# Mixer stage of a two-block transformer kernel: score products in pairs, two banks for transposes, convolution taps spread, gate projections moved to the last round, exponentials after the probability copies

## What is computed

```python
proj = einsum('bsd,dn->bsn', rmsnorm(x), w_in)      # qa ka va za | qb kb vb ob zb | gates | ga gb
# branch A, 4 heads, two components of 64 features each
scores = q @ k.T * d**-0.5 + alibi_bias             # causal, block of 128 queries
p = softmax(scores)
p = p[:, :, 0] - lam * p[:, :, 1]                   # difference of the two components
oa = p @ v
# branch B (mLSTM), 4 heads of 128 features; q and k first go through a causal convolution of 4 taps and silu
Sm = (q @ k.T) * Dm ; num = Sm @ v + w_inter * (q @ C) ; den = ...
h = num / max(|den|, exp(-m)) ; C = decay * C + (wk * k).T @ v
# both outputs are later normalised and multiplied by silu(za), sigmoid(ob), silu(zb)
```

## Time and profile before

| | us |
|---|---|
| median of 3 runs | 2411.23 |
| lowest, highest | 2407.95, 2414.12 |
| the profiled execution, its own time | 2416.63 |
| its span, first to last instruction | 2414.8 |
| mixer stage on PE, first to last projection product | 1326.0 to 2014.5 |

### The profile page before, as it was taken

How to read it: one execution, slowest core, us unless ns; L and a number is a source line. 1 busy time by engine, 2 the same in 40 slices (tenths; PEclk the granted TensorE clock), 3 DMA queues, 4 the chain that set the end, 5 groups by cost and what they waited for, 6 DMA issues and landing times. The chain is left out here.

```text
span 2414.8 us, 29418 instructions
## 1 busy us (share of the span) xinstructions
PE 2131.7 (88%) x11320; PEld 1673.9 (69%) x11320; DVE 1240.3 (51%) x2222; ACT 866.5 (36%) x1364; POOL 251.8 (10%) x159
## 2 busy tenths in 40 slices
PE   3589999999999999679993999999899887999998
PEld 1467878787878777557772866667676655788877
DVE  5658586775858595547445334224233231633453
ACT  2365353535343434147113132433333442520121
POOL 0220202020201111000002211111111100000000
PEclk7789999999999999789996999999999898999999
DMA  6123232322222232156112210120211104311232
GB/s 280 37 74 98 59 104 63 97 92 69 92 66 87 72 94 66 47 203 213 46 44 97 65 53 27 53 79 27 93 38 35 61 26 183 98 50 46 86 92 83
DMA packets 126523, 199.21 MB, mean 82 GB/s; under 512 B 56325, under 2 KB 87813, under 8 KB 125233
## 3 DMA queue, kind: packets, MB, share of 16 engines
q1 hardware_dynamic: 126384, 197.34, 25.2%
HBM read 155.17 MB, written 42.11 MB: 82 GB/s over the span
## 5 line engine op out<-in xcount | busy, mean ns | idle before, releaser
L709 PE MATMUL p_job<-h_hi,w_hi 128*128 128x512 f32 x784 | 332.7, 424 | 45.5 <-DVE w_lo L850 22.9
L710 PE MATMUL p_job<-h_lo,w_hi 128*128 128x512 f32 x784 | 313.1, 399 | 0.0
L711 PE MATMUL p_job<-h_hi,w_lo 128*128 128x512 f32 x784 | 312.1, 398 | 0.0
L1697 PE MATMUL m_job<-h_hi,m_hi 128*128 128x512 f32 x592 | 263.3, 445 | 36.7 <-POOL m_lo L1533 36.7
L1699 PE MATMUL m_job<-h_hi,m_lo 128*128 128x512 f32 x592 | 240.2, 406 | 0.0
L1698 PE MATMUL m_job<-h_lo,m_hi 128*128 128x512 f32 x592 | 239.6, 405 | 0.0
L709 PEld LDWEIGHTS p_job<-h_hi,w_hi 128*128 128x128 f32 x784 | 151.8, 194 | 88.6 <-DVE w_lo L850 23.1
L710 PEld LDWEIGHTS p_job<-h_lo,w_hi 128*128 128x128 f32 x784 | 151.7, 193 | 37.4 <-issue 8.5
L711 PEld LDWEIGHTS p_job<-h_hi,w_lo 128*128 128x128 f32 x784 | 151.6, 193 | 32.8
L1697 PEld LDWEIGHTS m_job<-h_hi,m_hi 128*128 128x128 f32 x592 | 115.8, 196 | 82.9 <-POOL m_lo L1533 37.3
L1533 POOL TENSOR_TENSOR m_lo<-m_raw,m_hi 128x1024 fp32r<-128x1024 f32 x37 | 89.8, 2428 | 467.2 <-DVE m_hi L1805 467.2
(11 more groups left out here) (357 smaller groups left out, 4356.2 us busy)
## 6 DMA issues: line engine op xcount, KB each, us to landing
w_raw<-in_w SPq DMA_DIRECT2D x49, 512.0 KB, 3.6
m_raw<-in_w SPq DMA_DIRECT2D x37, 512.0 KB, 3.6
rows<-grows SPq DMA_DIRECT2D x32, 512.0 KB, 6.4
ada<-in_ada_w SPq DMA_DIRECT2D x8, 1536.0 KB, 12.6
e_raw<-in_w SPq DMA_DIRECT2D x24, 512.0 KB, 3.7
z_scr<-pre SPq DMA_DIRECT2D x16, 512.0 KB
o_scr<-oT SPq DMA_DIRECT2D x64, 128.0 KB, 1.8
ob<-o_scr SPq DMA_DIRECT2D x16, 512.0 KB, 3.7
```

What stands on the lines that cost most here:

```text
L709: nc.tensor.matmul(p_job[h][:], hi, h_hi[:, k, cut], start=(k == 0), stop=False)
L710: nc.tensor.matmul(p_job[h][:], hi, h_lo[:, k, cut], start=False, stop=False)
L711: last = nc.tensor.matmul(p_job[h][:], lo, h_hi[:, k, cut], start=False, stop=(k == KD - 1))
L1697: nc.tensor.matmul(p_job[h][:], hi, h_hi[:, k, cut], start=(k == 0), stop=False)
```

## The change

Nothing of the arithmetic changes; what changes is order, buffers and engines.

- **Score products in pairs.** A score step was (t, component) with all keys of the block. Now it is (t, a) with a the half of 512 keys: both components are multiplied one behind the other, component c into bank c of `p_sc`. The row minimum of a block with two halves is the smaller of two, a DVE instruction more. Twelve score steps a head for sixteen, with weight 2 + t%4.
- **Two transpose banks.** `p_t` becomes two banks used in turn; a cols or turn step waits for the copy of the one before the previous. The second bank is that of `p_a`, which moves into columns 128 to 255 of the bank of `p_s`; so apply waits for the state update of its block, and sim for the copy of the previous apply.
- **Exponentials behind the copies.** Both exponentials of block t+1 are a step `exps` of their own after the turns of block t. The second turn of a block stands behind the second score of the next one.
- **Taps spread.** Each of the four taps of qb and kb is a step `tap` of its own, dealt out 1, 3, 5 and 7 slices after the job; its silu comes at 10 slices.
- **Gates.** Rounds 1 to 3 have two gate jobs each, round 4 has six: 128, 128, 128 and 96 slices for 144, 144, 144 and 48.
- **The low part of the weights** is made by DVE directly after the high part; POOL keeps one instruction a round (line 1546).

```diff
+GATE_SHARE = (0, 2, 2, 2, 6)
...
-        steps += [("score", 0, 0), ("score", 0, 1), ("sim", 0)]
-        for i in range(NT):
-            steps += [("blend", i)]
-            if i + 1 < NT:
-                steps += [("score", i + 1, 0), ("score", i + 1, 1)]
-            steps += [("update", i)]
-            steps += [("turn", i, q) for q in range((i + 4) // 4)]
-            steps += [("apply", i), ("out", i)]
+        steps += [("score", 0, 0), ("exps", 0), ("sim", 0)]
+        for t in range(NT):
+            steps += [("blend", t)]
+            steps += [("score",) + x for x in SCORES if x == (t + 1, 0)]
+            steps += [("update", t), ("turn", t, 0)]
+            steps += [("score",) + x for x in SCORES if x == (t + 1, 1)]
+            steps += [("turn", t, 1)] if t >= 4 else []
+            steps += [("exps", t + 1)] if t + 1 < NT else []
+            steps += [("apply", t), ("out", t)]
...
         if s[0] == "score":
-            return 2 + s[1] // 3
+            return 2 + s[1] % 4
...
+                        behind += [(1 + 2 * q, ("tap", j, q)) for q in range(TAPS)] + [(10, ("silu", j))]
...
-        p_t, p_a, p_s, p_u = ps("p_t"), ps("p_a"), ps("p_s"), ps("p_u")
+        p_t = [ps("p_t0"), ps("p_t1")]
+        p_s, p_u = ps("p_s"), ps("p_u")
+        p_a = p_s[:, P:2 * P]
...
-                def split_lo(J):
-                    pool.wait_ge(w_hi_done, J + 1)
-                    nc.gpsimd.tensor_tensor(w_lo[:, J % 2, :], w_raw[:], w_hi[:, J % 2, :].bitcast(F32),
-                                            ALU.subtract).then_inc(w_lo_done, 1)
...
+                        elif s[0] == "exps":
+                            t = s[1]
+                            w = (t + 1) * P
+                            if NT * g + t >= 2:
+                                act.wait_ge(rl_done, 2 * (NT * g + t) - 2)
+                            for c in range(2):
+                                if t >= 4:
+                                    act.wait_ge(mn_done, NT // 2 * g + t - 3)
+                                else:
+                                    act.wait_ge(sc_used, NSC * g + 2 * o[("score", t, 0)] + c + 1)
+                                nc.scalar.activation(sc[:, t % 2, c, 0:w], sc[:, t % 2, c, 0:w], ACT.Exp, scale=-1.0,
+                                                     bias=mn[:, t % 2, 0, c:c + 1], accum_out=ls[:, t % 2, c:c + 1]
+                                                     ).then_inc(exp_done, 1)
...
                         elif s[0] == "score":
...
-                            w = (t + 1) * P
-                            half = slice(DA * c, DA * (c + 1))
-                            for a in range(0, w, HALF):
-                                e = min(a + HALF, w)
-                                last = nc.tensor.matmul(p_sc[:, a:e], qa[half, g % 2, t * P:(t + 1) * P],
-                                                        ka[half, g % 2, a:e], start=True, stop=True)
-                            last.then_inc(sc_ready, 1)
+                            a0, e = a * HALF, min((a + 1) * HALF, (t + 1) * P)
+                            for c in range(2):
+                                half = slice(DA * c, DA * (c + 1))
+                                nc.tensor.matmul(p_sc[:, c * HALF:c * HALF + e - a0], qa[half, g % 2, t * P:(t + 1) * P],
+                                                 ka[half, g % 2, a0:e], start=True, stop=True).then_inc(sc_ready, 1)
                         elif s[0] == "turn":
...
-                            if o[s]:
-                                pe.wait_ge(turn_cp, m)
+                            if o[s] >= 2:
+                                pe.wait_ge(turn_cp, m - 1)
...
                         elif s[0] == "apply":
...
+                            pe.wait_ge(c_done, (NT + 1) * g + 2 + t)
...
                         elif s[0] == "sim":
...
+                                pe.wait_ge(app_cp, m)
...
-                def split_hi(J):
+                def split(J):
                     dve.wait_ge(w_in, 16 * (J + 1))
                     if J >= 2:
                         dve.wait_ge(half_done, 2 * (J - 1))
                     nc.vector.tensor_copy(w_hi[:, J % 2, :], w_raw[:]).then_inc(w_hi_done, 1)
+                    dve.wait_ge(w_hi_done, J + 1)
+                    nc.vector.tensor_tensor(w_lo[:, J % 2, :], w_raw[:], w_hi[:, J % 2, :].bitcast(F32),
+                                            ALU.subtract).then_inc(w_lo_done, 1)
```

More of the change, by code:

```diff
@@ L1315, in _, with mix_jobs, mix_plan @@
                 low(KD - 1)
[L1319 to L1327, removed]
+MIX_INPUTS = ("qa", "ka", "va", "qb", "kb", "vb")
+MIX_GATES = ("za", "ob", "zb")
+GATE_SHARE = (0, 2, 2, 2, 6)
+def mix_jobs():
+    gates = [(name, head) for head in range(HB) for name in MIX_GATES]
+    out = []
+    for i, n in enumerate(GATE_SHARE):
+        at = sum(GATE_SHARE[:i])
+        out.append(([(name, i) for name in MIX_INPUTS] if i < HB else []) + gates[at:at + n])
+    return out
+MIX_JOBS = mix_jobs()
+MIX_LIST = [("if", 0)] + [job for jobs in MIX_JOBS for job in jobs]
+MIX_AT = {job: J for J, job in enumerate(MIX_LIST)}
+SCORES = [(t, a) for t in range(NT) for a in range(t // 4 + 1)]
+def mix_plan(i):
+    recurs = i > 0
+    slices = [("slice", MIX_AT[job], h, k) for job in MIX_JOBS[i] for h in range(2) for k in range(KD)]
+    steps, behind = [], []
     if recurs:
@@ L1356, in send @@
     def send(upto):
-        nonlocal sent
+        nonlocal sent, behind
         while sent < min(upto, len(slices)):
@@ L1363, in send @@
             sent += 1
+            behind = [(n - 1, x) for n, x in behind]
+            out.extend(x for n, x in behind if n <= 0)
+            behind = [(n, x) for n, x in behind if n > 0]
             if s[3] == KD - 1:
@@ L1382, in mix_plan @@
     send(len(slices))
-    return out
+    return out + [x for n, x in behind]
 def stage_mix(nc, ctx, io, keep):
@@ L1498, in _ @@
                     for s in plans[i]:
-                        if s[0] == "weights" and 2 < job(i, s[1]) + 1 < N_JOBS:
-                            load(job(i, s[1]) + 1)
+                        if s[0] == "weights" and 2 < s[1] + 1 < N_JOBS:
+                            load(s[1] + 1)
                         elif s[0] == "bcast" and i < HB:
@@ L1768, in _ @@
                             for b in range(t + 1):
-                                last = nc.tensor.matmul(p_a[:, 0:P], va[:, b, :], PT[:, b, :], start=(b == 0), stop=(b == t))
+                                last = nc.tensor.matmul(p_a, va[:, b, :], PT[:, b, :], start=(b == 0), stop=(b == t))
                             last.then_inc(app_ready, 1)
@@ L2393, in _layout @@
     second = [[(0, gates2 + HB, HB), (32, gates2, HB)]]
-    for i in range(HB + 1):
-        second += [[(0, at2[name] + i * P, P)] for name in MIX_JOBS[:6] if i < HB]
-        second += [[(0, at2[name] + (i - 1) * P, P)] for name in MIX_JOBS[6:] if i]
+    second += [[(0, at2[name] + head * P, P)] for name, head in MIX_LIST[1:]]
     win2, cqk = a["w_in_2"][0], a["conv_qk_2"][0]
```

145 lines of the change are left out of this document (70 added, 75 removed).

## The result

The changed kernel takes 2319.66 us (median of 4 runs, 2315.74 to 2322.91) against 2409.59 us before (median of 4): a ratio of 0.9629, 95% interval 0.960 to 0.9657, so 90 us or 3.7% less. The forecast was 2345 us with 2322 to 2380: the direction was right, the gain was larger than the range allowed, by 2 us at its end and by 24 us at the forecast. The profiled execution took 2319.87 us, its span 2318.1 us against 2414.8.

A forecast was written before the change was run, and what follows sets the result against it. The prediction took PE's own work in the mixer stage, plus waits for ACT and DVE, as the bound. Terms -31 -20 -7 -3 -1 +6 -10 made -66 us from 2411, so 2345 us, range 2322 to 2380.

The forecast's parts named there:

- Clock: TensorE's slow clock after stalls in the mixer stage, priced at up to 38 us; -10 us of it was taken.
- Copies: Two transpose banks and exponentials behind the copies: -20 us of turn and apply waits, -7 us of column-copy waits.
- Scores: Paired score products of two components overlap on two array halves, saving half of 62 us: -31 us.
- the bound I had named as -34: Upper bound of the score gain, adding fewer switches between large and small tiles: -34 us; the other bound was 0.
- What line 789 showed for 32 columns: Products on two row groups started together there, the second costing nothing; taken as the value for the score pairs.
- The sign that I named for it: Score pair timeline: two times 0.43 us would show full overlap, three times partial overlap, four times none.
- the quarter case: Score passes start in program order, only the middle two overlap: -15 us for scores, -50 in all, 2361 us, chance 0.13.
- The charge for round 4: Moved gate stores make DVE wait for loads at four places in round 4, 1.5 us stall each: +6 us.
- rival D: Slower: DVE held 5.8 us at ten weight places following gate stores, stalling PE; +26 us, 2437 us, chance 0.06.
- Gates: Gate jobs moved to round 4: zero in itself, pays by covering that round's 20.9 us idle time, counted elsewhere.
- Low part, taps and silu: Low part on DVE: -1 us at stage entry; taps and silu spread: -3 us at the end of round 0.
- The low end of the range: 2322 us: adds -3 for switches, -10 of clock and -10 of waits to the sum of -66 us.

The follow-up runs named there:

- the undone run: Changed kernel with three gate jobs in each of rounds 1 to 4 instead of two, two, two and six: 2324.7 us, ratio 0.965.
- the later store: Changed kernel with SP's gate store issued three slices later, behind the load of the next weights: 2297.7 us, ratio 0.9543.

## Why the prediction was wrong

- **Clock, the term that failed.** "The stalls behind the copies go, the one at round starts gets shorter, the last block's stays. Of 38 us I take -10." By the clock columns slow time fell from 77 to 20 us, worth 28 by the same halving. Two steps of that sentence were wrong. First, the last block's stall did not stay: the waits for the blend in rounds 1 to 3 went from 7.4 us (three of 2.5) to 1.4 (three of 0.5), and with each went 6.8 us of slow clock, 20 us in all. What is left there is a wait for sm of 1.5 to 2.2 us without a slow stretch. These are the same places in round 2, before and after (length, busy, clock as in rows 2):

```profile
1726.00:1738.00 12.00, 10.52 (x46) 8.71 (x47) 3.10 (x15) 3.62 (x6) 0.00 (x0) 0.72 0.00 0
```

```profile
1660.00:1672.00 12.00, 11.63 (x66) 9.46 (x66) 3.53 (x17) 6.44 (x11) 0.00 (x0) 1.00 0.13 53
```

- **Clock at the round starts.** Second, the stall at a round's start did get shorter (14.0 and 4.0 to 7.8 and 0.7 us), but its slow stretch did not shrink in proportion. Read in steps of 2 us, the clock gives 27 us of slow time there before and 7 after; at the copies 10 and none, in the rest of round 4 14 and 10, at the stage's entry 6 and 4. I had counted stretches only for stalls that vanish. Of PE's idle stretches, 11 of 2.4 to 4.5 us held 34.5 of the 59 us before; after, two are left, 5.6 us. The slow stretches number 12 before (6.0 us in the mean, without the entry) and 5 after (3.4 each), and since some stand behind stalls of 2.0 to 2.3 us, a count of long stalls explains most of the term and not all.
- **Copies.** -20 for the copy waits and -7 for the columns were right as waits: 22.3 to 2.2 and 14.0 to 7.8. As a part of the change, copies and exponentials are worth 51 us, not 27 plus a share of 10, by their clock and by the minima (5.9 to 0.8), which I had left at their size.
- **Scores.** -31 was taken, -35 measured by the view (79.8 to 44.4): half of the passes and fewer switches, the bound I had named as -34. What line 789 showed for 32 columns carried over to 512. The sign that I named for it was off: a pair was to take 0.86 us, but a row has 0.23 us more than its passes, so 1.13 is full overlap. The rule of the Trainium skill that I weighed (TensorE: Matmul & The Clock Gate, Part 3, "What overlaps and what doesn't") didn't decide. By the quarter case the sum would have been 2361 us and the row 1.52 us; 1.13 speaks against reading its order pass by pass for fp32.
- **The charge for round 4**, +6, did not come: its idle time is 10.2 us for 20.9 with four gate stores in its way. But the mechanism is there, in rounds 1 to 3 (5.5 us of sm waits), and it is what rival D described; it cost 5.5 us of waits in the changed kernel where D had priced 58, and removing it gave 22 us.
- **Gates.** "It pays by covering round 4's idle time" was wrong as a reason: 5 us by the undone run, and zero once the store is out of the way.
- **Low part, taps and silu.** -1 and -3 were entry and round 0 alone; undone they cost 4.5 and 10 us, with 7.2 and 12.7 us more of waits for the blend. The taps stand in DVE's list ahead of it, and the low part on POOL stretches an instruction in front of it. The 2.17 us instruction in rows 7 had shown that, and I counted nothing for it.
- Against the terms: -35 of scores, -34 of waits (59.5 to 25.8; I had -25 in all) and -28 of clock are -97, within 2 us of the stage's 95.5. Short were the clock by 18, the waits by 9, the scores by 4. The low end of the range had added up 10 more of clock, 10 of waits and 3 of scores, so waits and scores stayed about within it; the clock alone went beyond, by 8 us. The profiled executions differ by 96.8 us and the medians by 90, and executions of before differ in clock too (0.947 at 2402.8 us, 0.941 at 2412.1), so some of the 28 us belongs to the profiled execution of before, which at 2416.6 us took longer than any of the four behind the median.

Not tried: whether two banks help without the later exponentials and without the pairing, and whether the low part and the taps are still worth 4.5 and 10 us behind the later store. Why the pairing alone brings a wait list longer than before's at the turns is open.

## What to carry to other kernels

Price the stalls of a matmul stage by length class, not by sum: twelve stalls of four microseconds cost a third more than their length here, twelve of two cost about themselves, so shortening a long one can pay more than the time cut from it. For lengths between them, look at the clock behind each stall instead of assuming. In an engine that works in order, look for the cheap instruction that another engine needs (a copy, a store) standing behind a long one (exponentials, a load's wait), and move it ahead; two earlier places of the exponentials cost 33 and 46 us here, and the doubled use of the array was worth 22 to some 32. When a moved piece of work pays, undo the move again after the next fix: the gates' share had been a remedy for a store in the wrong place.

## What the runs showed of the hardware

Two fp32 products with 64 rows each, on different halves of the array and into different banks, run at the same time at 512 columns: four passes take 1.13 us, where four on one half take 1.95, and the score line is busy 44.4 us for 79.8 before.

Twelve stalls of 2.03 us left the clock of TensorE at 0.98 to 1.00 by round, with a slow stretch behind three of them. Twelve of 3.9 to 4.9 us at the same places brought it to 0.89 to 0.97, with a slow stretch behind each. I had first priced the short ones as costing slow clock too.

A 128x1 product on DVE took 0.16 us in all of 32 cases while POOL did nothing but one instruction a round, and up to 2.35 us where POOL subtracted 128x1024 blocks.
